# Token groups of an expert visit taken in pairs, with 64-column stationaries, in a hybrid encoder layer with top-4-of-32 experts

## The reference, cut to what matters

```python
def moe_ffn(h, w_router, b_router, w_gate, b_gate, w_up, b_up, w_down, b_down):
    logits = (t @ w_router + b_router).astype(jnp.float32)
    top_val, top_idx = lax.top_k(logits, TOP_K)          # 4 of 32 experts a token
    top_w = jax.nn.softmax(top_val, axis=-1)
...
    def expert_block(args):
        xb, e = args
        g = xb @ w_gate[e] + b_gate[e]                   # 1024 x 1024
        u = xb @ w_up[e] + b_up[e]
        g = jnp.minimum(g, SWIGLU_LIMIT)
        u = jnp.clip(u, -SWIGLU_LIMIT, SWIGLU_LIMIT)
        act = g * jax.nn.sigmoid(SWIGLU_ALPHA * g) * (u + 1.0)
        return act @ w_down[e] + b_down[e]
...
    out = jnp.zeros_like(t).at[row_tok].add(ys * row_w[:, None].astype(t.dtype))
x = x + moe_ffn(rms_norm(x, norm_ffn[i]), ...)
```

## Time and profile before

| | us |
|---|---|
| median of three runs | 1386.47 |
| lowest and highest | 1384.63 and 1393.11 |
| the profiled execution, its own time | 1387.46 |
| its span, from first to last instruction | 1385.6 |
| TensorE busy | 1311.6 (95%) |
| VectorE, ScalarE, GpSimd busy | 459.1, 216.3, 206.5 |
| first product of the experts starts | 356.9 |
| last product ends | 1374.7 |

### The profile page before, as it was taken

The page is one execution under the profiler, slowest core; times in us unless marked ns, Lnnn a source line. Parts: engine busy times, 40 slices in busy tenths (PEclk is TensorE's granted clock), DMA queues, the critical chain, the costliest instruction groups (busy, mean ns, idle before and its releaser), DMA issues.

```text
span 1385.6 us, 40237 instructions
## 1 busy us (share of the span) xinstructions
PE 1311.6 (95%) x18054; PEld 796.2 (57%) x18054; DVE 459.1 (33%) x1059; ACT 216.3 (16%) x486; POOL 206.5 (15%) x152
## 2 busy tenths in 40 slices
PE   8999989998799999999999998999999998999994
PEld 3466665665456666666666655655655655666651
DVE  1875576654322223222222221221321321322310
ACT  2132243331101101110111110110010011001010
POOL 0031320000101221111112111121121121012121
PEclk9999999998799999999999999999999999999996
DMA  9200520146799999999999999999999999999994
GB/s 370 114 1 0 184 79 1 60 154 243 254 354 388 407 404 404 409 407 411 407 409 411 403 410 414 414 403 413 412 402 413 412 401 410 394 414 390 402 411 152
DMA packets 81342, 448.30 MB, mean 324 GB/s; under 512 B 14128, under 2 KB 22448, under 8 KB 32016
## 3 DMA queue, kind: packets, MB, share of 16 engines
q1 hardware_dynamic: 63936, 426.38, 75.5%
q0 software_dynamic: 16656, 17.20, 5.6%
q10 hardware_dynamic: 576, 2.10, 0.4%
HBM read 441.69 MB, written 14.94 MB: 330 GB/s over the span
## 4 chain that ended last, share of the span: by engine, by line
PE 55%; SPq 29%; DMA 6%; DVE 5%; issue 2%; ACT 1%; POOL 1%; POOLq 0%; ACTq 0%; DVEq 0%
PE pair L1958 34%; SPq L670 28%; PE pair L1794 4%; PE pair L1693 3%; PE pair L1654 3%; DMA ring<-in_w_up 3%; DMA ring<-in_w_down 2%; DVE rest L1120 2%; PE pair L1916 2%; PE pair L1649 1%; DVE rest L1151 1%; PE pair L1892 1%; PE pair L1929 1%; PE pair L1824 1%; PE pair L1784 1%
## 5 line engine op out<-in xcount | busy, mean ns | idle before, releaser
L1958 PE MATMUL pair<-ring,rest 128*32 128x256 f32 x14720 | 836.4, 382 | 29.1 <-DMA ring<-in_w_down 15.7
L1958 PEld LDWEIGHTS pair<-ring,rest 128*32 128x32 f32 x14720 | 469.6, 111 | 341.7 <-DMA ring<-in_w_down 19.9
L1120 DVE TENSOR_TENSOR rest<-pair,rest 128x512 f32<-128x512 f32 (+3 forms) x133 | 100.0, 755 | 441.5 <-PE pair L1958 406.8
L826 POOL DMA_INDIRECT out<-rest x82 | 128.4, 1566 | 752.2 <-ACT rest L1077 698.7
L1077 ACT ACTIVATE rest<-rest 128x256 f32<-128x256 f32 x82 | 36.5, 500 | 523.0 <-DVE rest L1120 523.0
L1059 ACT ACTIVATE rest<-rest 128x512 f32<-128x512 f32 (+3 forms) x34 | 24.4, 719 | 302.5 <-DVE rest L1471 302.5
L1693 PE MATMUL pair<-ring 128*128 128x512 f32 (+1 forms) x192 | 69.8, 523 | 0.0
L1120 DVE TENSOR_TENSOR rest<-rest 128x512 f32<-128x512 f32 (+8 forms) x85 | 56.6, 678 | 32.1 <-ACT rest L1059 26.7
L1438 DVE TENSOR_SCALAR rest<-pair,rest 96x1 int32<-96x1 f32 (+2 forms) x34 | 7.3, 215 | 176.0 <-issue 172.3
L1654 PE MATMUL pair<-ring 128*128 128x512 f32 x128 | 58.9, 620 | 6.2 <-DMA ring<-in_w_in 6.2
L1958 PE MATMUL pair<-rest 128*32 128x256 f32 x1024 | 62.3, 383 | 2.0 <-DMA rest<-in_w_down 2.0
(11 more groups left out here) (185 smaller groups left out, 867.6 us busy)
## 6 DMA issues: line engine op xcount, KB each, us to landing
ring<-in_w_gate SPq DMA_DIRECT2D x121, 1024.0 KB, 27.4
ring<-in_w_down SPq DMA_DIRECT2D x121, 1024.0 KB, 28.5
ring<-in_w_up SPq DMA_DIRECT2D x119, 1024.0 KB, 27.7
rest<-in_w_up SPq DMA_DIRECT2D x9, 1024.0 KB
rest<-in_w_gate SPq DMA_DIRECT2D x7, 1024.0 KB
rest<-in_w_down SPq DMA_DIRECT2D x7, 1024.0 KB
ring<-in_w_in SPq DMA_DIRECT2D x8, 520.0 KB, 8.3
ring<-in_x SPq DMA_DIRECT2D x8, 512.0 KB, 12.4
```

What stands on the lines that cost most here:

```text
L826: p.indirect_dma_start(out=out_rows, out_offset=bass.IndirectOffsetOnAxis(ap=sidx[vi.ring][:, g:g + 1].bitcast(I32), axis=0), in_=yrow_b[v ...
L1120: return v.tensor_tensor(out=out, in0=a, in1=b, op=op)
L1958: last = T.matmul(ps[q * TOK:(q + 1) * TOK, g * QW:(g + 1) * QW], x, pieces[slot][:, kk, q * QW:(q + 1) * QW], start=(k == 0 and g % 2 == ...
```

## The change

Within a visit the groups are taken in pairs. A pair is one stationary of 64 tokens, the matrix is cut into two halves of 512 columns instead of four quarters of 256, and there are two column groups of 64 (a *duo* of passes) instead of four of 32. The product of a pair and K tile is two matmuls instead of eight. The third group of a visit of three, and a single group, stay at 32 tokens and four quarters. So a visit of three has, in each K tile, first the two matmuls of its pair and then the four of its single group.

With that come: scatters of a pair as one DMA of 128 rows of 2 KB (48 scatters instead of 82); weights of the results for a pair in one instruction of 512 columns; a bias table in both layouts (three more gathers of 128 rows of 2 KB, at the start), and one bias row in place at a time, shuffled before each of the three uses; the gate written into the buffer of up, so that it waits for the transposes of the visit two back instead of for the sigmoid; `replicate` with two matmuls in a visit of three. The GpSimd drain at the end of the block is left out.

```diff
+PAIR, HW = 2 * TOK, 2 * QW
...
+        def pairs(vi):
+            return 0 if vi.j is None else vi.G // 2
+
+        def singles(vi):
+            return vi.G - 2 * pairs(vi)
+
+        def part_columns(vi):
+
+            p = pairs(vi)
+            return [(n, n * HW, HW) for n in range(p)] + [(p + n, p * HW + n * QW, QW) for n in range(singles(vi))]
...
-        block = ctx.enter_context(nc.Block())
+        block = ctx.enter_context(nc.Block(no_gpsimd_drain=True))
...
-                for g in range(vi.G):
+                for n, col, w in part_columns(vi):
                     p.indirect_dma_start(
-                        out=out_rows, out_offset=bass.IndirectOffsetOnAxis(ap=sidx[vi.ring][:, g:g + 1].bitcast(I32), axis=0),
-                        in_=yrow_b[vi.b][:, g * QW:(g + 1) * QW], in_offset=None, bounds_check=SEQ * NQ - 1, oob_is_err=False,
-                        compute_op=ALU.add).then_inc(s_scat, 16)
+                        out=out_halves if w == HW else out_rows,
+                        out_offset=bass.IndirectOffsetOnAxis(ap=sidx[vi.ring][:, n:n + 1].bitcast(I32), axis=0),
+                        in_=yrow_b[vi.b][:, col:col + w], in_offset=None, bounds_check=SEQ * (DM // w) - 1,
+                        oob_is_err=False, compute_op=ALU.add).then_inc(s_scat, 16)
...
+                p.indirect_dma_start(
+                    out=btab[:, (3 * m + 1) * QW:(3 * m + 3) * QW], out_offset=None, in_=bias_halves(m),
+                    in_offset=bass.IndirectOffsetOnAxis(ap=bias_i2.bitcast(I32), axis=0),
+                    bounds_check=NE * 2 - 1, oob_is_err=False).then_inc(s_btab, 16)
...
             def gate(vi, lk):
 
-                at_least(dve, s_sg, vi.n)
+                if back := before(vi, 2):
+                    wait_turned(dve, back.turns["a", last_part(back)])
+                gb, w = ub_b[vi.b], vi.G * QW
...
-                        for g in range(vi.G):
-                            col = TOK * (BLOCK_AT[g] if vi.G > 2 else g)
-                            x = xT[:, k, col:col + TOK] if m < 2 else aT[:, g, k % 2, k // 2, :]
-                            for q in range(NQ):
-                                last = T.matmul(ps[q * TOK:(q + 1) * TOK, g * QW:(g + 1) * QW], x,
-                                                pieces[slot][:, kk, q * QW:(q + 1) * QW],
-                                                start=(k == 0 and g % 2 == 0), stop=(k == KT - 1), skip_group_check=True)
+                        for n_, col, w in part_columns(vi):
+                            t0, tn = col * TOK // QW, w * TOK // QW
+                            if m < 2:
+                                x = xT[:, k, t0:t0 + tn]
+                            else:
+                                x = aT[n_][:, r % 2 * KP + kk, r // 2, :] if w == HW else aT[n_][:, kk, r, :]
+                            for q in range(DM // w):
+                                last = T.matmul(ps[q * tn:(q + 1) * tn, col:col + w], x,
+                                                pieces[slot][:, kk, q * w:(q + 1) * w],
+                                                start=(k == 0 and col % 512 == 0), stop=(k == KT - 1),
+                                                skip_group_check=True)
```

More of the change, by code:

```diff
@@ L150 @@
 C_REP = 7 * P
-C_GM = C_REP + P
-C_EPS = C_GM + MAX_GROUPS
+C_R64 = C_REP + P
+C_RSP = C_R64 + P
+C_GM = C_RSP + P
+C_EPS = C_GM + 2 + MAX_GROUPS
 C_ROW = C_EPS + 1
@@ L155 @@
 C_QB = C_Q4 + 1
-C_RK = C_QB + 1
+C_H2 = C_QB + 1
+C_HB = C_H2 + 1
+C_RK = C_HB + 1
 C_CAP = C_RK + 1
@@ L218, in constants @@
     row = np.arange(P)
[L219 to L220 removed]
+    c[:, C_REP:C_R64] = t % TOK == q % TOK
+    c[:, C_R64:C_RSP] = t % PAIR == q % PAIR
+    c[:, C_RSP:C_GM] = t == PAIR * (q % PAIR // TOK) + q % TOK
+    c[:, C_GM:C_GM + 2] = t // PAIR == q[:, 0:2]
+    c[:, C_GM + 2:C_EPS] = t // TOK == q[:, 0:MAX_GROUPS]
     c[:, C_FAR:C_TOK] = np.where(slot_rank[:, None] < TOK * np.arange(1, MAX_GROUPS + 1)[None, :], FAR, 3 * FAR)
@@ L225, in constants @@
     c[:, C_QB] = row // TOK
+    c[:, C_H2] = 2 * FAR + row // PAIR
+    c[:, C_HB] = row // PAIR
     c[:, C_RK] = np.array(RANK_AT)[row % NE]
@@ L318, in hybrid_layer @@
         fold_c = const[:, C_FOLD:C_COS]
-        rep_c, gm_c = const[:, C_REP:C_GM], const[:, C_GM:C_EPS]
+        rep_c, rep64_c, repsp_c = (const[:, n:n + P] for n in (C_REP, C_R64, C_RSP))
+        gm_c = const[:, C_GM:C_EPS]
         iota, far_c = const[:, C_IOTA:C_IOTA + NE], const[:, C_FAR:C_TOK]
         q4_c, qb_c, rk_c, cap_c, kcol_c = (const[:, n:n + 1] for n in (C_Q4, C_QB, C_RK, C_CAP, C_KCOL))
+        h2_c, hb_c = const[:, C_H2:C_H2 + 1], const[:, C_HB:C_HB + 1]
         gains = take((NH + NKV) * HD)
-        bias_w = rest[:, C_COS:C_END + (NH + NKV) * HD]
+        kT_w = take(NKV * SEQ)
+        btab = rest[:, C_COS:C_COS + 9 * QW]
+        at[0] = max(at[0], C_COS + 9 * QW)
         par = take(PAR)
@@ L350, in hybrid_layer @@
         qT = cut(qT_w, NH // 2, SEQ)
-        kT_w = take(NKV * SEQ)
         kT = cut(kT_w, NKV, SEQ)
@@ L392, in hybrid_layer @@
         wv = [take(MAX_GROUPS) for _ in range(8)]
-        bias_i = take(1)
+        bias_i, bias_i2 = take(1), take(1)
+        onehot_x = take(NT * TOK)
         hT_b = [xc_w[:, n * DM:(n + 1) * DM] for n in range(2)]
@@ L533, in hybrid_layer @@
         at_piece = {u: divmod(n, NRING) for n, u in enumerate(STREAM)}
-        scattered = [sum(VISITS[w][1] for w in range(v)) for v in range(NV + 1)]
+        scattered = [sum((VISITS[w][1] + 1) // 2 for w in range(v)) for v in range(NV + 1)]
+        def pairs(vi):
[5 more added lines that the diff above has]
+            return [(n, n * HW, HW) for n in range(p)] + [(p + n, p * HW + n * QW, QW) for n in range(singles(vi))]
         def visit(v):
@@ L1074, in weigh @@
                 wait_unit_taken(act, vi.units[2])
-                for g in range(vi.G):
-                    y = yrow_b[vi.b][:, g * QW:(g + 1) * QW]
-                    ins = nc.scalar.activation(y, y, ACT.Copy, scale=wv[vi.ring][:, g:g + 1])
+                for n, col, w in part_columns(vi):
+                    y = yrow_b[vi.b][:, col:col + w]
+                    ins = nc.scalar.activation(y, y, ACT.Copy, scale=wv[vi.ring][:, n:n + 1])
                 ins.then_inc(s_y, 1)
@@ L1477, in gated @@
                 w = vi.G * QW
-                lk(tt(sg_rows(vi)[:, 0:w], sg_rows(vi)[:, 0:w], gb[:, 0:w]))
+                lk(tt(sg_rows(vi)[:, 0:w], sg_rows(vi)[:, 0:w], ub_b[vi.b][:, 0:w]))
             def up(vi, lk):
-                if back := before(vi, 2):
-                    wait_turned(dve, back.turns["a", last_part(back)])
                 ub, w = ub_b[vi.b], vi.G * QW
@@ L1495, in down, with biases @@
                 plus_bias(vi, yrow_b[vi.b], 2)
-            def biases(j, a, b, lk):
-                lk(v.stream_shuffle(out=bias_x[:, a * QW:b * QW], in_=btab[:, a * QW:b * QW], mask=[j] * TOK))
+            def biases(j, m, lk):
+                lo = 0 if any(singles(vi) for vi in visit_at[j]) else QW
+                hi = 3 * QW if any(pairs(vi) for vi in visit_at[j]) else QW
+                lk(v.stream_shuffle(out=bias_x[:, lo:hi], in_=btab[:, 3 * m * QW + lo:3 * m * QW + hi], mask=[j] * TOK))
             (v0,), (v1,) = visit_at[0], visit_at[1]
@@ L1900, in replicate @@
                 c = spread(vi)
-                turned(T.matmul(ps[:, 0:2 * vi.G], rep_c[0:c, :],
-                                dmask[vi.b][0:c, 0:vi.G, :].rearrange("p a b -> p (a b)"), start=True, stop=True), use)
+                p, n = pairs(vi), pairs(vi) + singles(vi)
+                for a, b, copies in ((0, p, repsp_c if vi.G == 2 else rep64_c), (p, n, rep_c)):
+                    if a < b:
+                        last = T.matmul(ps[:, 2 * a:2 * b], copies[0:c, :],
+                                        dmask[vi.b][0:c, a:b, :].rearrange("p a b -> p (a b)"), start=True, stop=True)
+                turned(last, use)
             def kp_rows(ap, blocks):
```

68 lines of the change are left out of this document (42 added, 26 removed).

## The result

The changed kernel takes 1405.83 us (median of 4 runs, 1403.72 to 1408.08) beside 1388.05 us for the kernel before in the same series: ratio 1.0135, 95% interval 1.0108 to 1.0162. So the change costs 15 to 18 us. The forecast was +25.5 us: the sign and the range were right, the size was 8 us too large. The profiled executions differ by 16.8 us in span (1402.4 against 1385.6).

A forecast was written before the change was run, and what follows sets the result against it. TensorE was taken as the bound (or even with DMA) from 400 to 800 us, then DMA; 1387.46 + 31 (lateness) - 4.7 (drain) - 1 (DMA) = 1412.8, 1411.8 against the median, said as 1412; range 1379 to 1426.

The forecast's parts named there:

- what bounds the kernel: Whole kernel before: TensorE the bound, or even with DMA, from 400 to 800 us; DMA the bound from 800 to 1344.
- the price of a change: Three-group positions on TensorE: each change between 64 and 32 columns costs 0.15 us, 397 of them 59.6 us.
- the low bound of 0.118: Three-group positions: 0.118 us a change (46.8 us) if the load hides and only the emptying of the array stays.
- the drain: End of the block: without GpSimd's drain the barrier goes at 1380.7 us plus 0.2, -4.7 us.
- What of it reaches the end: After 800 us: of 59 us lateness 28 is taken up by TensorE's idle time, leaving +31 us, at most +37.
- DMA: DMA queues: larger scatter rows save 3 us (0 to 13), three bias gathers cost 2; -1 us in the sum.
- The first: Rival on TensorE: both widths share one configuration, no change costs anything; 1378 to 1379 us, or 1369; chance 16%.
- the second: Rival on TensorE: a change costs 0.09 to 0.11 us, the pair's stationary loading under the single group's streaming; 1395 us; chance 10%.
- The third: Rival in mixed K tiles: passes no longer side by side, a pair costs 1.72 instead of 0.86 us; near 1590; chance 3%.
- signs of being wrong: Profile after: the three-group K tile still takes 1.29 us, or TensorE waits at one place for VectorE or GpSimd.
- Pairing is neutral: TensorE, within the rival of free width changes: pairing itself gives only -2 us.
- scatters paid by the packet: DMA: if cost beyond the bytes goes by packet, larger rows save 13 us; 1369 us if width changes are also free.

The follow-up runs named there:

- no_drain_alone: The kernel before with only GpSimd's drain at the end of the block removed: 1380.84 us, ratio 0.9963 to the kernel before.
- changed_rows_1kb: The changed kernel with each pair's results scattered as two sets of 1 KB rows instead of one of 2 KB: 1411.45 us, ratio 1.0184 to the kernel before.
- threes_at_32: The changed kernel with visits of three kept at 32 columns and pairs only in visits of two and four: 1369.11 us, ratio 0.9877 to the kernel before.
- snake: The changed kernel with pair and single group in reverse order in every odd K tile, 229 changes of width: 1382.24 us, ratio 0.9971 to the kernel before.
- by_piece: The changed kernel taking both K tiles of a weight piece per width, order reversed every other piece, 121 changes: 1375.92 us, ratio 0.9924 to the kernel before.

## Why the prediction was right in sign and too large

**Right: what bounds the kernel.** TensorE full to 800 us (busy for 400.00 of the 400 us before it), DMA after (TensorE busy for 521.66 of 544, DMA share 1.00 to 1.02), and nearly all mixed visits in the part without slack: the prediction has them all before 784 us, but the down product of position 13 runs from 804.0 to 814.3 us in the kernel before.

**Right: the price of a change.** 0.15 us was taken from changes that are no 64-to-32 change; 0.144 was measured. It lay in the rows, but that this change would cost what the others do was a choice. That the array empties at a change, as the low bound of 0.118 supposes, no run shows. The K tile of three groups has the period forecast, 1.58 us. The lateness at position 15 was put at 59 us and is 56.2; of the difference 1.0 is that the changed kernel's products started 1.0 us earlier (355.9 against 356.9). Two slips in the working: the low bound takes off 0.024 us for the longer load, where rows 6 have 0.027, and by the sum it leads to 1399 us and not 1402. The GB/s of 365 to 385 came as 375 and 377.

**Right: the drain.** -4.7 us forecast. The time from the last scatter's issue to the end shrank by 5.1, and no_drain_alone measures 5.1 us (3 to 7). Of the 5.1 in the traces 0.6 is a quicker last landing, and 4.5 the drain and barrier.

**Mis-sized: "What of it reaches the end".** I took 22.3 us as used up before 1344 and 5.5 of the 11.1 after it, which is idle time alone. By the starts of the products, the lateness went from 56.2 at position 15 to 29.9 at position 30, so 26.3 was absorbed; from there to the last pass start it went to 20.1, another 9.8; the scatters then gave back 1.8. That is 34.3 us instead of 28.

The same work, from the gate product of position 15 to that of position 30, in the kernel before, after, and in changed_rows_1kb:

```profile
814.30:1314.10 499.80, 479.42 (x8069) 290.19 (x8062) 123.90 (x326) 53.81 (x111) 80.86 (x57) 0.99 1.02 406
```

```profile
870.50:1344.00 473.50, 472.42 (x2690) 184.75 (x2690) 140.66 (x357) 50.80 (x92) 51.04 (x38) 1.00 1.01 410
```

```profile
867.80:1341.20 473.40, 472.32 (x2690) 184.77 (x2690) 142.07 (x369) 50.94 (x92) 81.00 (x57) 1.00 1.02 409
```

The idle time fell from 20.4 to 1.1 us, which is 19.3, and the busy time by 7.0. And the last three products (up of position 31, down of 30 and 31), before and after:

```profile
1345.70:1374.70 29.00, 18.17 (x198) 6.84 (x190) 3.51 (x11) 1.20 (x3) 6.28 (x5) 0.71 0.71 247
```

```profile
1375.80:1394.80 19.00, 14.02 (x198) 7.67 (x190) 3.98 (x13) 1.20 (x3) 2.92 (x3) 0.82 0.82 299
```

The idle time fell from 10.8 to 5.0 us, so half of it counted, as the prediction took it, though for another reason: the waits for pieces went, and one of 4.98 us for ScalarE came. The rest is busy time, 18.17 to 14.02 us for the same 198 passes, at a mean granted clock of 0.71 before and 0.82 after. So the term that was too small is the slack: TensorE's busy time in the kernel before had 11.2 us in it that went away (7.0 up to position 30 and 4.2 in the tail), and the prediction counted idle time alone. In the tail most of this is the lower clock, by an estimate: at 0.50 TensorE was busy for 12.01 us before and 5.82 after, and 16 passes took 1.93 us at 0.50 and 1.07 at 1.00, so 0.86 of each 1.93 us is the clock's, 2.8 us of the difference of 6.19. Of the 7.0 us up to position 30 the pairs give 2.2 (432 pairs and K tiles x 0.005 us), and at 1155.8 us the clock was at 0.50 for 6.8 us, which didn't happen after; the rest is not taken apart. That the scatters wait for each other was right, but costs 1.8 us.

**Mis-sized, and without effect where it was looked for: "DMA", -1 us.** A row of 2 KB was taken as a saving of 3 us in a range of 0 to 13; the packets give 5.4. The reason given, that an accumulating row is read, added to and written, was the author's, and no run shows it; the packets show that it is more like the byte, 75 of the 101 ns of a 1 KB row. The instruction fetch was not in the sum at all, 4.9 us by its packets. So DMA was relieved of 10.3 us, less 2 for the bias gathers, where the sum had 3 less 2. But the changed kernel is paced by TensorE up to 1344 us, and with 1 KB rows it takes as long from position 15 to position 30 (473.4 against 473.5 us). The absorption there is TensorE's own slack and not the rows.

Of the 8.7 us between +25.5 and +16.8, 5.5 are the slack, 2.8 the lateness behind the three-group positions and 0.4 the end.

| step | forecast | by the two traces |
|---|---|---|
| late behind the last three-group position | +59 | +56.2 |
| absorbed up to position 30 (forecast: 22.3, and 1 for DMA) | -23.3 | -26.3 |
| absorbed in the tail, scatters' queue in it | -5.5 | -9.8 + 1.8 = -8.0 |
| drain and barrier | -4.7 | -5.1 |
| sum | +25.5 | +16.8 |

**The rivals.** None came. The first (no price) is refuted by the K tile; the second (0.09 to 0.11 us a change) would have led to 1395, and though the time lies half way to it, its mechanism is not what happened: the price was full, the slack larger. The third would have shown at once as a K tile of over 2 us. Of the signs of being wrong one half came: TensorE waits 1.2 us for VectorE (L1534) near 391 us, where it waited 1.4 before, and 4.98 us for ScalarE before the last product, which the prediction didn't have. "Pairing is neutral" stood in the first rival and was wrong as well: had changes of width been free, threes_at_32's 1369 us shows what would have come, the lower end that I gave to scatters paid by the packet, though the rows are worth some 4 to 5 us and not 13.

## What to carry to other kernels

Stationaries of 64 and 32 columns in one program were no loss here with 30 changes of width (threes_at_32), and a loss with 406 of them, most inside the K loop (the changed kernel, 1.0135): each change cost what a third of a 512-column pass costs (0.144 of 0.429 us). Group the work by width, or leave the odd part with its neighbours' width, as threes_at_32 does (0.987, faster than both kernels). Where DMA binds, count everything that its engines carry, the instruction fetch and the packets of scatters among it, and not only the weights. Where a late engine is to be absorbed by another's slack, follow the lateness from position to position and compare the same work before and after: the waits for weights in the tail went away when TensorE came later (10.8 us of idle time became 5.0), busy time fell beside them (by 4.2 us, an estimated 2.8 of it the lower clock), and another chain came out from behind them (the 4.98 us for ScalarE).

## What was unexpected of the hardware

- The instruction fetch stands among the DMA queues of the core's 16 engines (q8): 145 packets of 16 KB, 1.03 us each, 9.3 us of all engines for 40237 instructions. With half the instructions (20666) it was half, 68 packets and 4.4 us.
- An accumulating packet takes 101 ns for 1 KB and 176 ns for 2 KB; plain packets of queue 1 take 84 ns for 2 KB and 159 for 4 KB. By these sizes a KB more costs 75 ns where it is added and 37.5 where it is copied.
- The cost of a change of width is the same, with both directions taken together, in three orders of the same passes: 0.144 us in the mean of the changed kernel, 0.14 in snake and by_piece.
- The granted clock was lower behind waits of TensorE: in the kernel before, after waits of 1.22 and 2.15 us for pieces, it was 0.50 for 17.1 us, and 16 passes took 1.93 us instead of 1.07; it was 0.50 for 6.8 us from 1155.8 us on, after waits of 0.99 and 2.05 us. That the waits bring the lower clock no run shows.
